# Scaling of the softmax weights moved from VectorE to GpSimd in a two-layer attention kernel

## The chip, the cores and the metric

The kernel runs on one core of a Trainium2 chip. The metric is device time in microseconds, from start to end of one execution; the median of several runs is given. The core has five engines that run at the same time and wait for each other by semaphores: TensorE (PE in the profile; its weight loads are PEld), VectorE (DVE), ScalarE (ACT), GpSimd (POOL) and SyncE (SP), which here issues DMAs.

## What is computed

Two transformer layers on 256 rows of width 1024, in float32. The first layer attends with 16 query heads on 4 key/value heads in three branches (compressed blocks, selected blocks, window), each branch weighted by a gate:

```python
s = jnp.einsum('bqgrd,bgqkd->bgrqk', qc, kg).astype(jnp.float32) * scale
p = masked_softmax(s, msel)
o_sel = jnp.einsum('bgrqk,bgqkd->bqgrd', p.astype(vg.dtype), vg)
...
o = gc[..., 0:1] * o_cmp + gc[..., 1:2] * o_sel + gc[..., 2:3] * o_win
```

With 256 rows the selected branch and the window branch both come down to plain causal attention, with keys and values of their own. The second layer attends with 16 heads, each with its own keys and values, which comes down to causal attention as well. Each attention is followed by an output projection, a residual with layer norm, a gated feed-forward network of width 2816 and a second layer norm.

## The kernel before

All matrix products with weights are done as three products of a high part and a low part of each operand (L1050, `product`). ScalarE rounds each weight unit of 128 x 2048 (L427, through the helper at L420) and VectorE computes what is left of it (`rest_of_unit`, L700, through the helper at L698). Four such units are in flight; the units stream in by SyncE's DMAs. The order of the work on each engine is written out by hand, engine by engine, and the engines meet at counting semaphores.

Each attention runs in jobs: 16 in the first layer (8 pairs of heads, each with the selected and the window branch), 8 in the second (8 pairs of heads). A job handles two heads and both halves of the rows; the first half sees 128 keys, the second 256. So a job's weights are four blocks for each partition, of 128, 128, 256 and 256 columns, 768 in all. `probs` holds two jobs, so does the place of the scores in PSUM. What happens to job i:

- TensorE, `scores` (L1237 and the mask at L1241), after the exponential of job i-2 (`p_ready`)
- VectorE, `row_maxima` (L867): two reductions from PSUM
- ScalarE, `exp` (L561): four exponentials with their sums, after TensorE has turned job i-2 (`pT_done`)
- VectorE, `scale_probs` (L872 to L888): one reciprocal of the sums (L875), a wait for it on VectorE itself (`link`), and four multiplications in place, in the first attention by reciprocal and gate (L883), in the second by the reciprocal (L886)
- TensorE, `turn_probs` (L1252, L1256): six transposes, after `p_scaled`
- ScalarE copies the turned weights from PSUM (L584, shown as L420)
- TensorE, `weigh_values` (L1270, L1273, and in each second job of the first attention a product of the compressed branch, L1267)
- ScalarE and VectorE take the output of a pair of heads from PSUM as high and low part (`outputs_hi`, `outputs_lo`)

In each step i of its loop (L1280) TensorE does the scores of job i+2, then turns job i, then weighs the values of job i-1. In the last two steps there are no scores; twelve products with the output weights stand in their place. VectorE's loop (L902) does the maxima of job i+2, then `scale_probs` of job i+1, then `outputs_lo` of job i-2 where a pair of heads is complete. Ahead of the loop VectorE scales jobs 0 and 1. In the second attention 48 products of the last value projection stand between the scores of job 1 and those of job 2.

GpSimd makes constants at the start, loads the gains of the norms (`load_gain`, L387) and computes the reciprocal root of each variance (`roots`, L391, eight times in all); the rest of the time it waits. Its instructions stand in a fixed order (L401 to L412).

Of the kernel before, what the change touches and what calls it, by code (L numbers as in the profile page):

```python
# [26 lines left out]
HALF = 2  # L27
P = 128
# [26 lines left out]
NSA_JOBS = 16  # L55
MOBA_JOBS = 8
# [3 lines left out]
def build(nc, x_rows, x_cols, stream, w_gates, w1, w2, cpos, positions, norms, out):  # L60
# [4 lines left out]
    ALU = mybir.AluOpType  # L65
# [3 lines left out]
    with ExitStack() as ctx:  # L69
# [3 lines left out]
        def sem(name):  # L73
            return ctx.enter_context(nc.semaphore(name))
# [18 lines left out]
        probs = arena[:, 3072:4608].rearrange("p (b n) -> p b n", b=2)  # L93
# [28 lines left out]
        gates = sb("gates", [P, HALF, NH, 3])  # L122
        neg_max = sb("neg_max", [P, JOBS, HALF, 2])
        sums = sb("sums", [P, JOBS, HALF, 2])
        coef = sb("coef", [P, JOBS, HALF, 2])
# [69 lines left out]
        s_ready = sem("s_ready")  # L195
        max_ready = sem("max_ready")
        p_ready = sem("p_ready")
        p_scaled = sem("p_scaled")
        pT_done = sem("pT_done")
        pT_ready = sem("pT_ready")  # L200
# [141 lines left out]
        @block.gpsimd  # L342
        def _(gp):
            steps = [0]

            def link(ins):

                steps[0] += 1
                ins.then_inc(g_step, 1)
                gp.wait_ge(g_step, steps[0])  # L350

            nc.gpsimd.memset(minus_half[:, :], -0.5).then_inc(warm, 1)
            freqs = np.power(np.float32(THETA), -np.arange(0, ROPE, 2, dtype=np.float32) / np.float32(ROPE))
            for j in range(ROPE // 2):
                nc.gpsimd.memset(inv[:, j:j + 1], float(freqs[j]))
                nc.gpsimd.memset(inv[:, 8 + j:9 + j], float(freqs[j]))
            nc.gpsimd.memset(phase[:, :, 0:8], 0.0)
            nc.gpsimd.memset(phase[:, 0, 8:16], 0.25)
            nc.gpsimd.memset(phase[:, 1, 8:16], math.pi / 2)
            nc.gpsimd.memset(row_ok[:, :], 1.0)  # L360
            nc.gpsimd.memset(own_head[:, :], 1.0)
            nc.gpsimd.memset(causal[:, :, :], 0.0)
            nc.gpsimd.memset(cmp_mask[:, :, :], 0.0)
            nc.gpsimd.memset(hidT[:, :, :, :, :], 0.0)
            nc.gpsimd.memset(kcz[:, :, :, :], 0.0)
            nc.gpsimd.memset(hid_rows[:, :], 0.0)
            nc.gpsimd.memset(ident_b[:, :], 0.0)
            link(nc.gpsimd.memset(ident[:, :], 0.0))
            for m in (ident, ident_b):
                nc.gpsimd.affine_select(out=m[:, :], in_=m[:, :], compare_op=ALU.not_equal, fill=1.0, base=0,  # L370
                                        pattern=[[-1, P]], channel_multiplier=1)

            nc.gpsimd.affine_select(out=causal[:, :, :], in_=causal[:, :, :], compare_op=ALU.is_ge, fill=NEG,
                                    base=0, pattern=[[0, 2], [-1, P]], channel_multiplier=1)

            nc.gpsimd.affine_select(out=cmp_mask[:, :, :], in_=cmp_mask[:, :, :], compare_op=ALU.is_ge, fill=NEG,
                                    base=1 - CB, pattern=[[P, HALF], [-CS, 16]], channel_multiplier=1)

            nc.gpsimd.affine_select(out=row_ok[:, :], in_=row_ok[:, :], compare_op=ALU.is_ge, fill=0.0,
                                    base=1 - CB, pattern=[[P, HALF]], channel_multiplier=1)  # L380

            link(nc.gpsimd.affine_select(out=own_head[:, :], in_=own_head[:, :], compare_op=ALU.is_ge, fill=0.0,
                                         base=0, pattern=[[-16, 8]], channel_multiplier=1))
            nc.gpsimd.affine_select(out=own_head[:, :], in_=own_head[:, :], compare_op=ALU.is_ge, fill=0.0,
                                    base=15, pattern=[[16, 8]], channel_multiplier=-1).then_inc(consts, 1)

            def load_gain(l):  # L387
                gp.dma_start(gain[:, 0, :], norms[l, 0:1, :].to_broadcast([P, D])).then_inc(gain_in, 16)
                gp.dma_start(gain[:, 1, :], norms[l, 1:2, :].to_broadcast([P, D])).then_inc(gain_in, 16)

            def roots(l):  # L391
                for half in range(HALF):
                    gp.wait_ge(var_ready, 2 * l + half + 1)
                    nc.gpsimd.tensor_tensor(rstd[:, l, half:half + 1], var_eps[:, l, half:half + 1],
                                            minus_half[:, :], ALU.pow).then_inc(rstd_ready, 1)

            def rows_done(sets, doubled):
                gp.wait_ge(turned, sets)
                gp.wait_ge(twice_ready, doubled)

            rows_done(Q1 + 1, 2)  # L401
            load_gain(0)
            roots(0)
            gp.wait_ge(x_ready, 4)
            load_gain(1)
            roots(1)
            rows_done(MK1 + 1, 2)
            load_gain(2)
            roots(2)
            gp.wait_ge(x_ready, 12)  # L410
            load_gain(3)
            roots(3)  # L412
# [269 lines left out]
        def _(dve):  # L682
# [3 lines left out]
            def link(ins):  # L686

                steps[0] += 1
                ins.then_inc(v_step, 1)
                dve.wait_ge(v_step, steps[0])  # L690
# [109 lines left out]
            for kv, k in ((0, KC), (1, VC)):  # L800
                dve.wait_ge(turned, k + 1)
                for part in range(2):
                    lo = HD * part
                    src = ps[lo:lo + HD, 4 + 2 * kv:6 + 2 * kv, :].rearrange("p b (g n j) -> p j (b g) n", n=16, j=CS)
                    last = nc.vector.tensor_tensor(
                        blocks[lo:lo + HD, kv, :, :, :], src[:, :, :, part:part + NCMP],
                        cpos_sb[lo:lo + HD, kv, :].unsqueeze(2).unsqueeze(3).to_broadcast([HD, CS, KV, NCMP]), ALU.add)
# [53 lines left out]
            def attend(jobs, job, j0, a0, u):  # L861
                def row_maxima(i):
                    b = i % 2
                    dve.wait_ge(s_ready, j0 + i + 1)
                    for half in range(HALF):
                        keys = P * (half + 1)
                        last = nc.vector.tensor_reduce(  # L867
                            neg_max[:, j0 + i, half, :],
                            ps[:, s_bank(b, 0):s_bank(b, 1) + 1, P * half:P * half + keys], AX.X, ALU.max, negate=True)
                    last.then_inc(max_ready, 1)  # L870

                def scale_probs(i):  # L872

                    dve.wait_ge(p_ready, j0 + i + 1)
                    link(nc.vector.reciprocal(coef[:, j0 + i, :, :], sums[:, j0 + i, :, :]))  # L875
                    for half in range(HALF):
                        keys = P * (half + 1)
                        for h in range(2):
                            at = slice(2 * P * half + h * keys, 2 * P * half + (h + 1) * keys)
                            one_over_sum = coef[:, j0 + i, half, h:h + 1]  # L880
                            if j0 == 0:
                                gate = gates[:, half, i // 2 * 2 + h, 1 + i % 2:2 + i % 2]
                                last = nc.vector.tensor_scalar(probs[:, i % 2, at], probs[:, i % 2, at],  # L883
                                                               one_over_sum, gate, ALU.mult, ALU.mult)
                            else:
                                last = nc.vector.tensor_scalar(probs[:, i % 2, at], probs[:, i % 2, at],  # L886
                                                               one_over_sum, None, ALU.mult)
                    last.then_inc(p_scaled, 1)  # L888

                def outputs_lo(i):  # L890
                    t = job(i)[0]
                    dve.wait_ge(a_hi_ready, a0 + t + 1)
                    minus(a_lo[:, :, t, :], out_ps(t), a_hi[:, :, t, :].bitcast(f32)).then_inc(a_lo_ready, 1)

                row_maxima(0)
                if j0 == 0:
                    rest_to(u + 2)
                row_maxima(1)
                scale_probs(0)
                scale_probs(1)  # L900
                rest_to(u + 2)
                for i in range(jobs):  # L902
                    if i + 2 < jobs:
                        row_maxima(i + 2)
                    if 0 < i and i + 1 < jobs:
                        scale_probs(i + 1)
                    if i >= 2 and job(i - 2)[4]:
                        outputs_lo(i - 2)
                    if i >= jobs - 2:
                        rest_to(u + 3 + i - (jobs - 2))  # L910
                for i in range(jobs - 2, jobs):
                    if job(i)[4]:
                        outputs_lo(i)
# [600 lines left out]
```

## Time and profile before

| | |
|---|---|
| median of 3 runs | 655.66 us (655.51 to 655.67) |
| profiled execution | 655.48 us, of which the span of the trace is 653.7 us |
| TensorE busy | 641.7 us, 98% of the span |
| VectorE busy | 400.3 us, 61% |
| ScalarE busy | 313.3 us, 48% |
| GpSimd busy | 16.3 us, 3% |
| granted clock of TensorE | 0.996 of full speed (2.4 GHz) |
| first attention | from about 79 to 136 us of the span |
| second attention | from about 402 to 440 us |

In the rows below, times are in microseconds from the start of the span unless marked ns. `arena` is the memory that holds `probs` and `probsT`; `ps` is PSUM. "out<-in" gives the tensors that are written and read, with partitions x elements and type; xN is the number of instructions that a row merges. "L883" is line 883 of the kernel. What stands in brackets at the end is the time that the engine was idle before the instruction, and what ended it; "issue" is time in which it waited for nothing that the profile shows. TensorE's products overlap each other, so a duration of one product is longer than its share of the time.

### The profile page before, as it was taken

The page shows a single profiled execution, that of the slowest core. Times are in us where ns is not written, and L with a number is a line of the kernel's source. Part 1 is how long each engine was busy: PE and PEld are TensorE (multiplying, and loading weights), DVE is VectorE, ACT ScalarE, POOL GpSimd, SP SyncE. Part 2 cuts the span into 40 slices and gives each one's busy share as a digit, 9 for nine tenths or more (in the row PEclk, how much of TensorE's full clock was granted, in tenths as well). Part 3 has the DMA queues.
Part 4 walks back from the last instruction along what each step waited for, and adds up shares of the span by engine and source line. Part 5 has one row for each costly group of instructions (what it writes and reads, how often), then busy time and mean ns, then how long its engine had stood idle before and what let it go on. Part 6 is the DMA issues. An engine that isn't in the chain of part 4 may idle for free.

```text
span 653.7 us, 8507 instructions
## 1 busy us (share of the span) xinstructions
PE 641.7 (98%) x3277; PEld 512.8 (78%) x3277; DVE 400.3 (61%) x505; ACT 313.3 (48%) x440; POOL 16.3 (3%) x56
## 2 busy tenths in 40 slices
PE   9999999999999999999999999999999999999995
PEld 6887766687888888888877887778788888888874
DVE  4794688868565445554477755787685445554437
ACT  5663588835443333444443555784263333444420
POOL 2000000001000000000000000000100000000001
PEclk9999999999999999999999999999999999999998
DMA  8993330035574545554533654313566555455301
GB/s 307 394 343 140 128 129 1 3 128 207 207 259 182 189 183 188 192 192 192 189 133 130 257 183 138 129 70 124 195 217 250 185 189 188 192 192 192 128 1 64
DMA packets 18718, 113.03 MB, mean 173 GB/s; under 512 B 2816, under 2 KB 3328, under 8 KB 6016
## 3 DMA queue, kind: packets, MB, share of 16 engines
q1 hardware_dynamic: 16528, 102.65, 42.6%
q10 hardware_dynamic: 1008, 5.77, 2.3%
q0 software_dynamic: 1152, 4.19, 1.9%
q8 instruction: 21, 0.34, 0.2%
q14 instruction: 9, 0.07, 0.0%
HBM read 111.56 MB, written 1.05 MB: 172 GB/s over the span
## 4 chain that ended last, share of the span: by engine, by line
PE 89%; DVE 9%; ACT 2%; issue 0%; DVEq 0%; ACTq 0%
PE ps L1052 25%; PE ps L1054 24%; PE ps L1053 24%; PE ps L1237 3%; DVE w_lo L698 2%; PE ps L1270 2%; PE ps L1252 2%; PE ps L1336 2%; DVE bn L933 1%; DVE x L947 1%; DVE x L928 1%; PE ps L1178 1%; PE ps L1134 1%; PE ps L1241 1%; DVE x L955 1%; PE ps L1119 1%
## 5 line engine op out<-in xcount | busy, mean ns | idle before, releaser
L698 DVE TENSOR_TENSOR w_lo<-raw,w_hi 128x2048 fp32r<-128x2048 f32 (+2 forms) x101 | 220.1, 2185 | 101.7 <-ACT w_hi L420 101.4
L1052 PE MATMUL ps<-w_hi,a_hi 128*128 128x512 f32 x592 | 235.4, 398 | 0.1
L420 ACT ACTIVATE w_hi<-raw 128x2048 fp32r<-128x2048 f32 (+2 forms) x101 | 184.3, 1830 | 97.6 <-PE ps L1054 89.6
L1054 PE MATMUL ps<-w_hi,a_lo 128*128 128x512 f32 x592 | 231.0, 390 | 0.0
L1053 PE MATMUL ps<-w_lo,a_hi 128*128 128x512 f32 x592 | 230.7, 390 | 0.0
L1052 PEld LDWEIGHTS ps<-w_hi,a_hi 128*128 128x128 f32 x592 | 111.3, 188 | 24.1 <-issue 1.5
L1054 PEld LDWEIGHTS ps<-w_hi,a_lo 128*128 128x128 f32 x592 | 111.1, 188 | 23.8
L1053 PEld LDWEIGHTS ps<-w_lo,a_hi 128*128 128x128 f32 x592 | 111.4, 188 | 21.7
L1052 PE MATMUL ps<-w_hi,h_hi 128*128 128x512 f32 x160 | 62.4, 390 | 0.0
L1054 PE MATMUL ps<-w_hi,h_lo 128*128 128x512 f32 x160 | 62.3, 390 | 0.0
L1053 PE MATMUL ps<-w_lo,h_hi 128*128 128x512 f32 x160 | 62.2, 389 | 0.0
L607 ACT ACTIVATE arena<-ps 128x512 f32<-128x512 f32 x18 | 10.8, 599 | 68.3 <-PE ps L1054 68.3
L420 ACT ACTIVATE h_hi<-ps 128x512 fp32r<-128x512 f32 x20 | 12.0, 599 | 60.2 <-PE ps L1336 60.2
L561 ACT ACTIVATE arena<-ps,neg_max 128x128 f32<-128x128 f32 (+1 forms) x96 | 39.5, 448 | 2.3 <-DVE neg_max L867 2.3
L987 DVE TENSOR_TENSOR arena<-arena,ps 128x512 f32<-128x512 f32 x18 | 12.4, 688 | 37.8 <-ACT arena L607 37.8
L1054 PEld LDWEIGHTS ps<-w_hi,h_lo 128*128 128x128 f32 x160 | 30.0, 188 | 6.3
L1052 PEld LDWEIGHTS ps<-w_hi,h_hi 128*128 128x128 f32 x160 | 30.0, 188 | 6.2
L1053 PEld LDWEIGHTS ps<-w_lo,h_hi 128*128 128x128 f32 x160 | 30.0, 188 | 6.2
L420 ACT ACTIVATE arena<-ps 128x768 f32<-128x768 f32 (+2 forms) x28 | 23.6, 847 | 21.4 <-PE ps L1054 12.0
L698 DVE TENSOR_TENSOR h_lo<-ps,h_hi 128x512 fp32r<-128x512 f32 x20 | 13.8, 691 | 28.5 <-ACT h_hi L420 28.5
L867 DVE TENSOR_REDUCE neg_max<-ps 128x2 f32<-128x256 f32 (+1 forms) x48 | 24.4, 553 | 8.0 <-PE ps L1241 7.5
L420 ACT ACTIVATE a_hi<-ps 128x256 fp32r<-128x256 f32 (+1 forms) x28 | 13.8, 501 | 20.0 <-PE ps L1087 17.9
(150 smaller groups left out, 475.5 us busy)
## 6 DMA issues: line engine op xcount, KB each, us to landing
raw<-stream SPq DMA_DIRECT2D x94, 1024.0 KB, 4.8
arena<-w ACTq DMA_DIRECT2D x4, 1024.0 KB, 13.8
rows<-norms POOLq DMA_DIRECT2D x8, 512.0 KB, 4.6
twice<-x_cols SPq DMA_DIRECT2D x4, 256.0 KB, 6.1
raw<-stream SPq DMA_DIRECT2D x2, 512.0 KB, 7.3
x<-x_rows ACTq DMA_DIRECT2D x1, 1024.0 KB, 5.0
out<-x SPq DMA_DIRECT2D x3, 256.0 KB, 2.1
raw<-stream ACTq DMA_DIRECT2D x2, 256.0 KB, 4.3
```

Of the source, the lines that this page charges most:

```text
L420: return nc.scalar.activation(dst, src, ACT.Copy, scale=scale)
L561: last = nc.scalar.activation(probs[:, b, at:at + keys], ps[:, s_bank(b, h), P * half:P * half + keys], ACT.Exp, bias=neg_max[:, j0 + i, h ...
L698: return nc.vector.tensor_tensor(dst, a, b, ALU.subtract)
L867: last = nc.vector.tensor_reduce(neg_max[:, j0 + i, half, :], ps[:, s_bank(b, 0):s_bank(b, 1) + 1, P * half:P * half + keys], AX.X, ALU.ma ...
L987: nc.vector.tensor_tensor(h_rows[:, :, :], silu[:, :, :], ps[:, 0:2, FC:2 * FC], ALU.mult).then_inc(h_ready, 1)
L1052: nc.tensor.matmul(dst, hi, m_hi, start=start, stop=False)
L1053: nc.tensor.matmul(dst, hi, m_lo, start=False, stop=False)
L1054: return nc.tensor.matmul(dst, lo, m_hi, start=False, stop=stop)
L1237: nc.tensor.matmul(ps[:, s_bank(b, h), P * half:P * half + keys], qT[on, q, P * half:P * (half + 1)], kk[on, k, 0:keys], start=half == 0, ...
L1252: nc.tensor.transpose(acc_flat[:, 2048 + P * (2 * h + half):2048 + P * (2 * h + half + 1)], probs[:, b, at:at + P], ident[:, :])
L1270: nc.tensor.matmul(dst[HD * h:HD * (h + 1)], values[:, 0, cols[h]:cols[h] + HD], probsT[:, b, S * h:S * (h + 1)], start=j0 > 0, stop=False)
L1336: last = nc.tensor.transpose(hT_ps[:, half, t, :], h_rows[:, half, P * t:P * (t + 1)], ident[:, :])
```

## The change

A new semaphore `coef_ready` counts reciprocals. VectorE's part of the step becomes `reciprocals`: the same wait for the exponential, the reciprocal, and a signal; the wait of VectorE for its own reciprocal goes. The four multiplications, with the same operands, are now issued by GpSimd in a loop over all jobs of an attention, with one wait for the reciprocal for each job and the signal `p_scaled` at the job's last multiplication. In GpSimd's order they stand after the load of gain 0 and ahead of root 0 in the first attention, and after the load of gain 2 and ahead of root 2 in the second.

```diff
+            def scale_probs(jobs, j0):
+                for i in range(jobs):
+                    gp.wait_ge(coef_ready, j0 + i + 1)
+                    for half in range(HALF):
+                        keys = P * (half + 1)
+                        for h in range(2):
+                            at = slice(2 * P * half + h * keys, 2 * P * half + (h + 1) * keys)
+                            one_over_sum = coef[:, j0 + i, half, h:h + 1]
+                            if j0 == 0:
+                                gate = gates[:, half, i // 2 * 2 + h, 1 + i % 2:2 + i % 2]
+                                last = nc.gpsimd.tensor_scalar(probs[:, i % 2, at], probs[:, i % 2, at],
+                                                               one_over_sum, gate, ALU.mult, ALU.mult)
+                            else:
+                                last = nc.gpsimd.tensor_scalar(probs[:, i % 2, at], probs[:, i % 2, at],
+                                                               one_over_sum, None, ALU.mult)
+                    last.then_inc(p_scaled, 1)
...
             rows_done(Q1 + 1, 2)
             load_gain(0)
+            scale_probs(NSA_JOBS, 0)
             roots(0)
...
             load_gain(2)
+            scale_probs(MOBA_JOBS, NSA_JOBS)
             roots(2)
...
-                def scale_probs(i):
+                def reciprocals(i):
 
                     dve.wait_ge(p_ready, j0 + i + 1)
-                    link(nc.vector.reciprocal(coef[:, j0 + i, :, :], sums[:, j0 + i, :, :]))
...
-                    last.then_inc(p_scaled, 1)
+                    nc.vector.reciprocal(coef[:, j0 + i, :, :], sums[:, j0 + i, :, :]).then_inc(coef_ready, 1)
...
                 row_maxima(1)
-                scale_probs(0)
-                scale_probs(1)
+                reciprocals(0)
+                reciprocals(1)
                 rest_to(u + 2)
                 for i in range(jobs):
                     if i + 2 < jobs:
                         row_maxima(i + 2)
                     if 0 < i and i + 1 < jobs:
-                        scale_probs(i + 1)
+                        reciprocals(i + 1)
```

## Rows read from the trace of the kernel before

**Rows 1.** The page: busy time of each engine, share of the span, instructions.

```profile
PE 641.7 (98%) x3277; PEld 512.8 (78%) x3277; DVE 400.3 (61%) x505; ACT 313.3 (48%) x440; POOL 16.3 (3%) x56
```

**Rows 2.** Busy time by stretch: stretch, its length, each engine, clock, DMA.

```profile
92.34:125.90 33.56, 33.56 (x291) 22.42 (x291) 29.27 (x88) 30.14 (x113) 0.00 (x0) 1.00 0.01 1
419.00:430.70 11.70, 11.70 (x107) 7.75 (x105) 10.52 (x35) 11.70 (x46) 0.00 (x0) 1.00 0.01 4
```

**Rows 3.** Timeline, first attention's middle: start, duration, engine, line, operation.

```profile
102.79 0.93 PE L1237 MATMUL ps<-kk,qT 64*128 64x128 f32 x8
...
103.25 0.42 DVE L698 TENSOR_TENSOR a_lo<-ps,a_hi 128x256 fp32r<-128x256 f32 x1
...
104.08 1.02 DVE L867 TENSOR_REDUCE neg_max<-ps 128x2 f32<-128x256 f32 x2 [0.41 <-PE ps L1241]
...
105.02 0.17 DVE L875 RECIPROCAL coef<-sums 128x4 f32<-128x4 f32 x1
...
105.22 1.25 DVE L883 TENSOR_SCALAR arena<-arena,coef,gates 128x128 f32<-128x128 f32 x4
...
105.42 0.93 PE L1237 MATMUL ps<-kk,qT 64*128 64x128 f32 x8
...
106.52 0.66 PE L1252 MATMUL ps<-ident,arena 128*128 128x128 f32 x4
...
108.56 0.93 PE L1237 MATMUL ps<-kk,qT 64*128 64x128 f32 x8
```

**Rows 4.** Timeline, start of the first attention.

```profile
86.48 1.73 ACT L420 ACTIVATE arena<-ps 128x1024 f32<-128x1024 f32 x2
86.64 0.18 DVE L875 RECIPROCAL coef<-sums 128x4 f32<-128x4 f32 x1 [0.42 <-ACT arena L561]
...
86.85 1.25 DVE L883 TENSOR_SCALAR arena<-arena,coef,gates 128x128 f32<-128x128 f32 x4
...
88.01 1.95 DVE L867 TENSOR_REDUCE neg_max<-ps 128x2 f32<-128x256 f32 x4
...
89.07 0.37 ACT L561 ACTIVATE arena<-ps,neg_max 128x128 f32<-128x128 f32 x1 [0.85 <-DVE neg_max L867]
...
90.82 0.18 DVE L875 RECIPROCAL coef<-sums 128x4 f32<-128x4 f32 x1 [0.86 <-ACT arena L561]
...
92.34 0.66 PE L1252 MATMUL ps<-ident,arena 128*128 128x128 f32 x4 [0.25 <-DVE arena L883]
```

**Rows 5.** Timeline, second attention, jobs 2 to 4.

```profile
419.83 0.18 DVE L875 RECIPROCAL coef<-sums 128x4 f32<-128x4 f32 x1 [0.26 <-ACT arena L561]
...
419.90 0.93 PE L1237 MATMUL ps<-kk,qT 64*128 64x128 f32 x8
...
421.11 0.66 PE L1252 MATMUL ps<-ident,arena 128*128 128x128 f32 x4
```

**Rows 6.** Timeline of GpSimd and the variance before its first root.

```profile
2.27 0.32 POOL L366 MEMSET hid_rows<- 128x256 f32 x1
2.52 0.20 POOL L367 MEMSET ident_b<- 128x128 bf16 x1
2.67 0.20 POOL L368 MEMSET ident<- 128x128 f32 x1
3.11 0.29 POOL L370 TENSOR_SCALAR_AFFINE_SELECT ident<-ident 128x128 f32<-128x128 f32 x1 [0.24 <-POOL ident L368]
3.37 0.29 POOL L370 TENSOR_SCALAR_AFFINE_SELECT ident_b<-ident_b 128x128 bf16<-128x128 bf16 x1
3.62 0.41 POOL L373 TENSOR_SCALAR_AFFINE_SELECT causal<-causal 128x256 bf16<-128x256 bf16 x1
3.98 0.21 POOL L376 TENSOR_SCALAR_AFFINE_SELECT cmp_mask<-cmp_mask 128x32 f32<-128x32 f32 x1
...
143.27 0.15 DVE L940 TENSOR_SCALAR var_eps<-mean_var 128x1 f32<-128x1 f32 x1
...
143.51 1.00 POOL L394 TENSOR_TENSOR rstd<-var_eps,minus_half 128x1 f32<-128x1 f32 x1 [68.08 <-DVE var_eps L940]
```

More of the change, by code:

```diff
@@ L197, in build @@
         p_ready = sem("p_ready")
+        coef_ready = sem("coef_ready")
         p_scaled = sem("p_scaled")
@@ L870, in row_maxima @@
                     last.then_inc(max_ready, 1)
-                def scale_probs(i):
+                def reciprocals(i):
                     dve.wait_ge(p_ready, j0 + i + 1)
-                    link(nc.vector.reciprocal(coef[:, j0 + i, :, :], sums[:, j0 + i, :, :]))
[L876 to L887, printed above, removed]
-                    last.then_inc(p_scaled, 1)
+                    nc.vector.reciprocal(coef[:, j0 + i, :, :], sums[:, j0 + i, :, :]).then_inc(coef_ready, 1)
                 def outputs_lo(i):
```

## The prediction

> **What bounds the kernel now.** I read the busy line of each engine first. TensorE is busy for 641.7 us of the 653.7 us span, 98% [rows 1]. So a change on VectorE or GpSimd pays only where TensorE now waits for it, and costs only where TensorE comes to wait. The change touches the two attention stretches alone. The busy times of stretches say that in the middle of both, TensorE is busy all the time (33.56 of 33.56 us, and 11.70 of 11.70 us), that ScalarE is close to it (30.14, and 11.70), that VectorE has some rest, and that GpSimd does nothing [rows 2]. There is nothing to gain in the middle: the row maxima wait for scores, not the other way round.
>
> The timeline of two jobs in the middle of the first attention shows who waits for whom [rows 3]. Call S(n) the scores of job n, T(n) the turning of its scaled weights, V(n) its weighted values. TensorE runs S(n+1), T(n-1), V(n-2), S(n+2), T(n), in this order. S starts at 102.79, 105.42 and 108.56: periods of 2.63 and 3.14, the longer one with the extra product of the compressed branch in it. T starts 1.10 after its S (105.42 to 106.52), and from T to the next S it is 1.53 (103.89 to 105.42), or 2.04 with the extra product (106.52 to 108.56).
>
> Now the way to T(n) beside TensorE: S(n+1) starts at 102.79, its maxima at 104.08 (1.29 later), the reciprocal of job n at 105.02 to 105.19 (2.40 after S), the four scalings of job n at 105.22 for 1.25, to 106.47. T(n) starts at 106.52, 0.05 later, which is also just when TensorE is done with S(n+2). So every second job of the first attention has a slack of about nothing: this is the place that decides. The other jobs have the 0.5 us that the extra product gives. The reciprocal cannot come sooner, since VectorE puts the maxima of job n+1 ahead of it, and they wait for TensorE.
>
> **The change part by part.** What goes: 96 scalings leave VectorE, 1.25 us a job in the first attention. What comes: a semaphore from VectorE to GpSimd, the same scalings there, and GpSimd's signal to TensorE. The first hop: the variance ends at 143.42 and GpSimd's root starts at 143.51, so 0.09 [rows 6]. For the last hop I take the 0.05 of VectorE. With X for the four scalings of a job on GpSimd, T(n) can start 2.40 + 0.09 + X + 0.05 = 2.54 + X after S(n+1). Now it starts 3.73 after it. So X is covered up to 1.19, call it 1.2 us. Write e = X - 1.2.
>
> In the first attention, when e is above 0, T(n) of an odd job is late. After it come 2.04 to S(n+3), and again 2.54 + X to T(n+2): a pair takes 4.58 + X instead of 5.78, which is e more. The even job between has its slack and rides along. This is one e a pair, not one a job. It holds for T(5), T(7), T(9), T(11) and T(13): 5e. T(3) is set by T(2), below. T(14) and T(15) have twelve matmuls of the output weights ahead of them, and cost nothing.
>
> *Start of the first attention* [rows 4]. Here VectorE is now in the way: scaling job 1 holds it from 86.85 to 88.10, and the maxima of jobs 2 and 3 start only at 88.01. ScalarE's exponential of job 2 starts at 89.07 after 0.85 of waiting; its copies had ended at 86.48 + 1.73 = 88.21. With the scalings gone, the maxima of job 2 can start at 86.82 (after the reciprocal) and end at 87.84, ahead of ScalarE's copies. The exponential then starts at 88.21, 0.86 sooner, and with it the reciprocal of job 2 (90.82 now) and S(4). T(2), now at 92.34, would start at 90.82 - 0.86 + 0.18 + 0.09 + X + 0.05 = 90.28 + X: at X = 1.2 it is 91.48, a gain of 0.86. So the start gives -0.86 + e, once. T(3) then follows T(2) by TensorE's own 2.64. T(0) and T(1) move by up to e as well; S(4) then follows V(0) at about 90.3 + e, and from that side T(2) could start at 91.4 + e, no later than from the other.
>
> *Second attention* [rows 5]. Jobs 0 and 1 are scaled long before T(0), under a block of 48 matmuls. At T(2) VectorE isn't held up by anything: the reciprocal starts at 419.83 because the exponential ended, and the scaling ends just before T(2) at 421.11. Here the hop is pure addition: 419.83 + 0.18 + 0.09 + X + 0.05 = 420.15 + X, at X = 1.2 421.35, a loss of 0.24. T(4) adds another e as above (all periods are short ones here, so T(n) late by e gives T(n+1) its slack back). T(6) and T(7) are covered by matmuls. Together 0.24 + 2e.
>
> *Other queues.* GpSimd's waits stand in order: the gain loads are issued ahead of the scalings as before, its roots come 10 us after the last scaling, so nobody waits for what is queued behind. The 24 new signals from VectorE replace a wait of VectorE on itself. VectorE's output parts come sooner, and TensorE didn't wait for them.
>
> *The price X.* The trace has no tensor_scalar on GpSimd. Its memsets advance by 0.15 us (128 columns) and 0.25 (256), so four such would take 0.15 + 0.15 + 0.25 + 0.32 = 0.87: a floor, since nothing is read. Its selects, which read one tensor and write one, advance by 0.26 and 0.36 and end after 0.41: 0.26 + 0.26 + 0.36 + 0.41 = 1.29 [rows 6]. A select of 128 columns takes 0.29, a memset 0.20: reading one operand adds 0.09. The new scalings read two scalars of each partition from SBUF besides (one in the second attention). My estimate is 0.09 for each: X = 1.29 + 4 x 0.18 = 2.01 in the first attention, 1.29 + 4 x 0.09 = 1.65 in the second. The ceiling is the root: 1.00 for one column, so four of these are 4.0. I stay near the selects, since the ceiling is a power, not a product.
>
> The Trainium skill (GPSIMD Engine Reference, § Performance pitfalls for Q7 kernels) puts about 102 cycles on each read command, which at its 1.2 GHz is 0.085 us; the trace's 0.09 between select and memset agrees. Its opening speaks against the change as a whole: for elementwise arithmetic VectorE is roughly twice as fast. By that, X would be 2 x 1.25 = 2.5; no row here shows it, and the sum would be that of rival (b) at its near edge.
>
> **The sum.** First attention: e = 0.81, -0.86 + 0.81 + 5 x 0.81 = +4.0. Second: e = 0.45, 0.24 + 0.9 = +1.1. Together +5.1 us. The profiled execution took 655.48 us with 1.8 around its span; the median of the runs shown is 655.66, 0.18 above. On the median: 660.8 us.
>
> With one X for both, the change is -0.62 + 8e. Ends: X = 0.87 gives e = -0.33. Then the middle is TensorE's own, and so is the start from T(1) on, at 88.10 by T(0) after S(2): T(2) comes at 91.3, a gain of 1.0. The second attention gains 0.1 (S(4) is the limit): -1.1 in all, 654.5. X = 4.0 gives 8 x 2.8 - 0.6 = +21.8; GpSimd's own queue, 4.1 a job, is not yet worse than that.
>
> **The rivals.** (a) GpSimd is as quick as its selects or quicker, the two scalars cost nothing: X from 0.87 to 1.44. At 1.29 the sum is +0.1, 655.8 us; at 1.2 it is 655.0. The start's gain then pays for the second attention's hop. This is the case on the other side: its place is T(2) of the first attention, its price 0.86, and it decides as long as e stays under 0.08. For it: both select rows, and a single pass over one tensor. Against it: the fixed 0.09 for an operand.
>
> (b) Arithmetic on GpSimd costs twice VectorE's 1.25 or more: X from 2.5 to 4.0. At X = 2.5 the sum is -0.6 + 10.4 = +9.8, 665.4 us; at 4.0 it is 677.5. For it: the root at 1.00 us for one column, a large fixed price. Against it: that is a power, and the selects are not dear.
>
> (c) The two engines exclude each other at SBUF. The output part of VectorE (0.42 us at 103.25 [rows 3]) follows right behind each second reciprocal, so exactly beside a scaling. In the first attention it falls on the even jobs, whose 0.5 covers it only if X is small; at my X it would move them by up to 0.42 + 0.81 - 0.50 = 0.73, which the next odd job then has as slack. In the second it comes with jobs 3 and later and adds about 0.4. Some 1 us in all, to 661.8: inside my range. The Trainium skill (SBUF — State Buffer, § Who interferes with whom) holds only VectorE instructions with two SBUF inputs or in a 2-port mode to block GpSimd; the output part has one input from PSUM. By that rule (c) costs nothing, and only the rests of whole weight units (two SBUF inputs) count, which fall where matmuls cover them.
>
> (d) The diff does what it says: no wait of VectorE for the scaled weights remains, so I give no chance to a change without effect.
>
> **How the numbers follow.** My case (X from 1.44 to 2.5, with or without (c)): 0.55. Rival (a): 0.28. Rival (b): 0.17. What a measurement of this kernel can tell from no change is about 0.2%, 1.3 us; it is crossed at e = 0.24, X = 1.44, upwards. Downwards no X reaches it: 0.03, taken out of (a), stands for a use of VectorE's free time that I don't see. So faster 0.03, within 0.25, slower 0.72. The range starts at 655.0, the X at which the cover just holds, which leaves out the lower part of (a), and goes to 668.0, X = 2.8, which takes in the near half of (b).
>
> **What would show it.** GpSimd rows of 128 and 256 columns near 0.45 and 0.57 us (no stretch where they are 0.3 and 0.4). TensorE's L1252 released by GpSimd in every second job, S to S twice summing to 4.6 + X rather than 5.78. The maxima of job 2 at about 86.8, T(2) at 90.3 + X. VectorE idle most of each job. I am wrong if L1252 never waits (X below 1.2), if it waits in every job by the whole of e, or if the pair of periods grows while X is below 1.2, which would mean a longer hop.

## The result, and the profile after

The changed kernel takes 664.07 us (median of 4 runs, 663.78 to 665.49) against 655.65 us for the kernel before: a ratio of 1.0133, with a 95% interval of 1.0121 to 1.0146. It is 8.4 us slower. One of the four runs, at 665.49, had a mean granted clock of 0.994, the other three 0.997. The forecast was 660.8 us with a range of 655.0 to 668.0: the sign and the range hold; 5.1 us were forecast and 8.4 measured.

The page of the kernel after: busy time, and the chain that ended last by engine. GpSimd, which was busy for 16.3 us [rows 1] and in neither attention, now has 76.7 us and 3% of the chain.

```profile
PE 643.4 (97%) x3277; PEld 512.6 (77%) x3277; DVE 372.9 (56%) x409; ACT 313.6 (47%) x440; POOL 76.7 (12%) x152
...
PE 84%; DVE 9%; POOL 3%; ACT 2%; issue 1%; DMA 1%; DVEq 0%; ACTq 0%
```

Busy time by stretch: T(2) to T(13) of the first attention, and the second attention from 420 to 436 us. TensorE, busy all the time before [rows 2], is busy for 32.66 of 35.49 us and for 12.61 of 16.00 us. VectorE, relieved, only became idle.

```profile
92.84:128.33 35.49, 32.66 (x274) 20.91 (x274) 13.91 (x40) 28.09 (x106) 21.39 (x44) 1.00 0.00 1
...
420.00:436.00 16.00, 12.61 (x110) 8.10 (x112) 6.60 (x17) 11.78 (x41) 11.30 (x17) 1.00 0.21 89
```

GpSimd's scalings by line and shape (line, engine, operation, count, busy us, mean ns): first the first attention's form (L408, reciprocal and gate) over the whole span, then the second's (L411, reciprocal alone) from 424 to 438 us, where nothing disturbs them.

```profile
L408 POOL TENSOR_SCALAR arena<-arena,coef,gates 128x256 f32<-128x256 f32 x32 | 17.4, 553 | 0.0
...
L408 POOL TENSOR_SCALAR arena<-arena,coef,gates 128x128 f32<-128x128 f32 x32 | 14.0, 446 | 27.2 <-DVE coef L895 27.2
```

```profile
L411 POOL TENSOR_SCALAR arena<-arena,coef 128x256 f32<-128x256 f32 x8 | 7.3, 922 | 0.0
L411 POOL TENSOR_SCALAR arena<-arena,coef 128x128 f32<-128x128 f32 x8 | 4.7, 602 | 4.7 <-DVE coef L895 4.7
```

The form with *less* arithmetic takes longer. The four scalings of a job take 1.95 us in the first attention and 2.97 in the second (5.94 for two jobs back to back). Over the whole span the mean of the second's short ones is 0.85 and that of the long ones 1.02, the numbers that the expectations below go by: a few instructions that VectorE blocked are in those means (see the last section).

Where the 8.4 us lie is read from GpSimd's first root of each norm. It starts at 148.00 instead of 143.51 after the first attention; the profiled execution was already 0.16 later before the first scaling (the maxima of job 0 at 80.79 instead of 80.63), so the first attention costs 4.33 us. Between the fourth root and the fifth it is 104.96 us (351.96 to 456.92) instead of 100.78 (347.50 to 448.28): the second costs 4.18. Together that is 8.51.

Some 0.35 us come back in a place that the change does not touch. Behind the sixth root (463.12 before, 471.76 after), VectorE's next step of the norm starts 1.70 us after the root in the kernel before and 1.36 after it in the changed one. At the other seven roots it is 1.34 or 1.35 in both.

```profile
464.82 1.42 DVE L955 SCALAR_TENSOR_TENSOR x<-x,rstd,rows 128x512 f32<-128x512 f32 x2 [0.46 <-DVE x L947]
```

```profile
473.12 1.41 DVE L962 SCALAR_TENSOR_TENSOR x<-x,rstd,rows 128x512 f32<-128x512 f32 x2
```

From the sixth root to the seventh it takes 179.25 us before and 178.91 after. All ten kernels of this document that scale the first attention on GpSimd, wholly or in part, take 178.9; the one other experiment on the kernel before ("early half alone", below) takes 179.27. The cause was not found. So 0.35 us are in the total time of each of the ten when it is compared with the kernel before.

### The profile page after: what moved, and what is told of

Same layout as the page of the kernel before. It is cut to its first block, busy times and chain, and to the rows that moved or that the text cites. A ratio compares the mean times of both kernels' runs of the same rounds, so it can differ in the third digit from the quotient of the medians.

```text
span 662.1 us, 8507 instructions
## 1 busy us (share of the span) xinstructions
PE 643.4 (97%) x3277; PEld 512.6 (77%) x3277; DVE 372.9 (56%) x409; ACT 313.6 (47%) x440; POOL 76.7 (12%) x152
## 4 chain that ended last, share of the span: by engine, by line
PE 84%; DVE 9%; POOL 3%; ACT 2%; issue 1%; DMA 1%; DVEq 0%; ACTq 0%
PE ps L1059 24%; PE ps L1061 24%; PE ps L1060 24%; DVE w_lo L718 2%; POOL arena L408 2%; PE ps L1343 2%; PE ps L1244 1%; POOL arena L411 1%; PE ps L1259 1%; DVE bn L940 1%; DVE neg_max L887 1%; PE ps L1277 1%; DVE x L954 1%; DVE x L935 1%; PE ps L1185 1%; DVE x L962 1%
## 5 line engine op out<-in xcount | busy, mean ns | idle before, releaser
L395 POOL TENSOR_TENSOR rstd<-var_eps,minus_half 128x1 f32<-128x1 f32 x8 | 8.0, 995 | 415.9 <-DVE var_eps L947 415.9
L408 POOL TENSOR_SCALAR arena<-arena,coef,gates 128x128 f32<-128x128 f32 (+1 forms) x64 | 31.1, 499 | 27.2 <-DVE coef L895 27.2
```

Source lines behind the costliest of these rows:

```text
L408: last = nc.gpsimd.tensor_scalar(probs[:, i % 2, at], probs[:, i % 2, at], one_over_sum, gate, ALU.mult, ALU.mult)
```

## The experiments

Each kernel was timed beside the kernel before, which took 655.57 to 655.64 us. "Changed kernel" means the one above, and every diff is against it unless it says otherwise.

### Each attention by itself

In the first run, the second attention's scalings go back to VectorE; the first attention stays on GpSimd.

```diff
-            scale_probs(MOBA_JOBS, NSA_JOBS)
...
+                    if j0 == 0:
+                        nc.vector.reciprocal(coef[:, j0 + i, :, :], sums[:, j0 + i, :, :]).then_inc(coef_ready, 1)
+                        return
+                    link(nc.vector.reciprocal(coef[:, j0 + i, :, :], sums[:, j0 + i, :, :]))
...
```

> The scalings of the first attention on GpSimd, those of the second back on VectorE. My theory: the two attentions cost separately, 4.3 us in the first (variance of the first norm 4.49 us later, less 0.16 of an offset at the start) and 4.2 in the second. So 655.65 + 4.3 = 660.0 us. Rival: part of the cost lies outside them, in a later stage that the shift disturbs; then the sum would not split so, and this kernel would be off 660.0 by over 0.5 us.

Measured: 659.54 us (659.43 to 659.61), 3.9 above the kernel before, ratio 1.0059 (1.0043 to 1.0076). The root stands at 147.91 in its profile, 4.40 later than before, and the second attention is back at 100.73 us between its roots (351.85 to 452.58). So the costs of the two attentions are separate. The time is 0.46 us below the 660.0 that were expected, just inside the 0.5 allowed, and the 0.35 gained behind the sixth root is most of that: a small part of the difference does lie outside the attentions, as a gain.

### Why the second attention's scalings are slow

Three kernels change nothing but the form of the instruction. The first two give the second attention a second multiplication, by a column of ones read from SBUF or by a constant in the instruction.

```diff
-                                                               one_over_sum, None, ALU.mult)
+                                                               one_over_sum, ones[:, 0:1], ALU.mult, ALU.mult)
...
-                                                               one_over_sum, None, ALU.mult)
+                                                               one_over_sum, 1.0, ALU.mult, ALU.mult)
```

> As the changed kernel, but in the second attention each scaling has a second multiplication, by a column of ones read as a scalar of each partition. Theory 'form': GpSimd runs the form with one operation slower (0.85 and 1.02 us) than the form with two (0.45 and 0.55); the added operation makes it faster, X falls from 2.97 to 1.95, and the second attention costs 0.24 + 2 x 0.75 = 1.7 instead of 4.2 us: 661.6 us. Rival 'stage': something of the second attention slows GpSimd; then its rows stay at 0.85 and 1.02 or rise, and the time is 664.1 or more.

> As the run with the column of ones, but the second factor is the constant 1.0 in the instruction. Theory 'two operations are the quick form': rows at 0.45 and 0.55 or 0.09 less each, since one scalar fewer is read; 661.0 to 661.6 us. Rival 'both factors have to be pointers to be quick': rows at 0.85 and 1.02, 664.1 us.

The third takes the gate out of the first attention.

```diff
-                                                               one_over_sum, gate, ALU.mult, ALU.mult)
+                                                               one_over_sum, None, ALU.mult)
```

> As the changed kernel, but the first attention leaves the gate out, so its scalings have one operation as in the second (the branches are then not weighted by their gates). Theory 'form': rows of 0.85 and 1.02 in the first attention too, X = 2.97; a pair of jobs takes 4.58 + 2.97 = 7.55 instead of 6.53, five pairs 5.1 more, the start about 1.5 more, the two longer turns of GpSimd's own queue some more: 671 us. Rival 'stage': rows stay at 0.45 and 0.55 or fall by 0.09 for the scalar that isn't read; 664.1 down to 662.

Measured: 661.36 us (661.24 to 661.55) with the column, 660.73 (660.65 to 660.82) with the constant, 672.79 (671.84 to 673.73) without the gate. The first is inside what was expected, the second 0.3 us below it. The groups by line and shape, first of the kernel with the constant 1.0 (second attention):

```profile
L411 POOL TENSOR_SCALAR arena<-arena,coef 128x256 f32<-128x256 f32 x16 | 7.4, 477 | 0.0
L411 POOL TENSOR_SCALAR arena<-arena,coef 128x128 f32<-128x128 f32 x16 | 5.7, 370 | 18.8 <-DVE coef L895 18.8
```

and then of the kernel without the gate (first attention):

```profile
L407 POOL TENSOR_SCALAR arena<-arena,coef 128x256 f32<-128x256 f32 x32 | 30.9, 979 | 0.0
L407 POOL TENSOR_SCALAR arena<-arena,coef 128x128 f32<-128x128 f32 x32 | 19.0, 606 | 21.6 <-DVE coef L894 21.6
```

The added multiplication makes the instruction 1.6 times (0.602 to 0.370) and 1.9 times (0.922 to 0.477) faster, and taking one out makes the first attention's as slow as the second's had been; four advance by 2.99 us there. So the form decides, not the stage. From 128 to 256 columns the two-operation form grows by 0.107 us, 0.84 ns a column, and the one-operation form by 0.32 us, 2.5 ns a column; extended to no column, an estimate, 0.26 and 0.28 are left. It is the price of a column that differs. With the constant, four scalings take 1.62 us; with the column of ones 1.96, the same as with the gates. The difference, 0.34 for four instructions, is the price of reading one more scalar of each partition: 0.085 each, where the prediction took 0.09 [rows 6]. Why GpSimd is slower at one operation than at two was not found; no run here looks inside it.

The run without the gate is 1.8 us above what was expected of it. Its four times fall in two groups: 671.84 and 671.96 us at a mean granted clock of 0.998, 673.61 and 673.73 at 0.995. The profile is of the 673.61. Busy time of stretches of it, three pairs of jobs and a part of the middle one; the last column but two is the granted clock.

```profile
110.87:118.44 7.57, 5.93 (x54) 3.83 (x50) 2.52 (x7) 5.12 (x20) 5.95 (x9) 1.00 0.00 0
118.44:127.58 9.14, 7.49 (x54) 4.70 (x50) 2.52 (x7) 5.11 (x20) 5.94 (x8) 0.81 0.01 3
122.00:125.00 3.00, 3.00 (x16) 1.64 (x14) 0.00 (x0) 2.30 (x9) 2.38 (x4) 0.50 0.03 8
127.58:135.15 7.57, 5.92 (x55) 3.84 (x50) 2.52 (x7) 5.12 (x20) 5.95 (x8) 1.00 0.00 0
```

The granted clock is 0.50 of full speed, 1.2 GHz, for about 3.4 us from 121.9. TensorE had waited for GpSimd for 1.65 us until 121.48. The pairs around it have waits of the same length (5.93 and 5.92 us busy of 7.57) at full clock, so a wait of this size does not always bring the fall. GpSimd's scalings, 7.57 us apart from pair to pair, are 9.14 apart there: 1.6 us, once. No other trace of this document has such a fall inside an attention. In the two executions at 0.998 it is presumably missing; they lie 0.9 us above what was expected, and that part is not explained.

### The order on VectorE

The kernel with the constant, and VectorE's loop takes the reciprocal first.

```diff
+                    if 0 < i and i + 1 < jobs:
+                        reciprocals(i + 1)
                     if i + 2 < jobs:
                         row_maxima(i + 2)
-                    if 0 < i and i + 1 < jobs:
-                        reciprocals(i + 1)
```

> The kernel with the constant 1.0 (660.7 us), and VectorE's loop takes the reciprocal of job i+1 ahead of the maxima of job i+2 instead of behind them; nothing is added or left out. My theory of the place that decides: T(n) is late because the reciprocal waits behind the maxima of the next job, which wait for TensorE. With the reciprocal first, T(n) can start 0.04 + 0.17 + 0.09 + X + 0.05 after the exponential of job n, about 2.3 at X = 1.95, and the pair of jobs in the first attention falls from 6.53 to between 5.85 and 6.06 us; the maxima come later, which costs the second attention up to 0.4 a job. 658.2 to 659.2 us. Rival: the length of the scalings on GpSimd alone sets the pair, whatever the order on VectorE; then the pair stays at 6.53 and the time at 660.7 or above it.

Measured: 657.19 us (657.09 to 657.88), 3.5 us below the same kernel with the old order, and 1.0 below the lower end of what was expected. Timeline of this kernel in the middle of the first attention:

```profile
104.52 0.60 PE L1259 MATMUL ps<-ident,arena 128*128 128x128 f32 x4
...
104.96 0.18 DVE L895 RECIPROCAL coef<-sums 128x4 f32<-128x4 f32 x1 [1.46 <-ACT arena L581]
105.05 0.99 DVE L887 TENSOR_REDUCE neg_max<-ps 128x2 f32<-128x256 f32 x2
105.23 1.96 POOL L408 TENSOR_SCALAR arena<-arena,coef,gates 128x128 f32<-128x128 f32 x4 [0.91 <-DVE coef L895]
...
107.25 0.66 PE L1259 MATMUL ps<-ident,arena 128*128 128x128 f32 x4
```

The reciprocal is released by ScalarE's exponential, not by the maxima, and 1.96 us on GpSimd end at 107.19, before T. T comes at 101.41, 107.25, 113.02 and 118.85: 5.81 a pair on average, where it was 6.53 in the changed kernel. The first attention then costs 0.67 us (root at 144.25, less 0.07 of offset) instead of 4.35. So most of the cost of the first attention can be had back with GpSimd as slow as it is. It hung on where GpSimd's work began: behind a reduction that waits for TensorE. The expected price in the second attention, 0.4 a job, was too high: it costs 1.30 between its roots (348.21 to 450.29), with the old order 1.10.

### Both engines at once

Each job's scalings are divided: those of 128 columns on GpSimd (in the second attention with the column of ones as second factor), those of 256 on VectorE; TensorE waits for both.

```diff
-                    for half in range(HALF):
+                    for half in range(1):
                         keys = P * (half + 1)
                         for h in range(2):
...
+                    dve.wait_ge(coef_ready, j0 + i + 1)
+                    for h in range(2):
+                        at = slice(2 * P + h * 2 * P, 2 * P + (h + 1) * 2 * P)
...
+                    last.then_inc(p_scaled_v, 1)
```

> Each job's four scalings are split: the two of 128 columns on GpSimd (two operations each, 0.45 us), the two of 256 columns on VectorE (0.41 us each), both at the same time. Theory 'they run beside each other': T(n) can start 2.40 + 0.09 + 0.87 + 0.05 = 3.41 after S(n+1), earlier than now with all on VectorE (3.73), so nothing is late and the start of the first attention gains some 0.3 us: 655.2 us. Rival 'they exclude each other at SBUF' (rival c of the prediction): rows of one of them stretch to the sum, 0.87 + 0.82, T(n) comes 0.5 late once a pair, 655.6 + 3 to 4 = 659 us.

Measured: 654.52 us (654.26 to 655.14), ratio 0.9982 (0.9973 to 0.9992): 1.1 us faster than the kernel before, and 0.7 faster than expected. By the roots it gains 0.94 us in the first attention, where 0.3 was expected, and loses 0.19 in the second (100.97 between its roots); the 0.35 behind the sixth root makes up the rest. Timeline of one job of this kernel:

```profile
104.44 0.17 DVE L898 RECIPROCAL coef<-sums 128x4 f32<-128x4 f32 x1
...
104.64 0.79 DVE L905 TENSOR_SCALAR arena<-arena,coef,gates 128x256 f32<-128x256 f32 x2
104.70 1.04 POOL L411 TENSOR_SCALAR arena<-arena,coef,gates 128x128 f32<-128x128 f32 x2 [2.02 <-DVE coef L898]
...
105.93 0.60 PE L1275 MATMUL ps<-ident,arena 128*128 128x128 f32 x4
```

They do run beside each other, but not freely: two scalings of 128 columns take 1.04 on GpSimd here, where two of the changed kernel would take 0.89, while VectorE's two take 0.79 as ever. GpSimd lost 0.15 of 0.79 us, not all of it, and both end before T. T follows its S by 1.09 (104.84 to 105.93), TensorE's own time.

Two more kernels keep the division in the first attention only, the second of them with an early half of the maxima of job 2; a third divides both attentions, with the constant in the second; a fourth is the kernel before with the early half alone.

```diff
                 reciprocals(0)
+                if j0 == 0:
+                    row_maxima(2, (0,))
                 reciprocals(1)
...
-                        row_maxima(i + 2)
+                        row_maxima(i + 2, (1,) if j0 + i == 0 else (0, 1))
```

> The split of the run before (128 columns on GpSimd, 256 on VectorE) in the first attention only; the second has all scalings on VectorE as in the kernel before the change. The split gained 0.9 us in the first attention and lost 0.2 in the second by the places of the roots, so 655.6 - 1.1 = 654.5 or a little less. Rival: the gain of 1.1 came from somewhere else in the kernel (the second attention, code positions); then this is back above 655.

> As the split in the first attention only, and in its start VectorE takes the first half of the maxima of job 2 (128 keys, 0.36 us) ahead of the reciprocal of job 1, where it is idle for 0.87 us. The exponential of job 2 then starts 0.3 us sooner (the copies on ScalarE end 0.4 us before it starts now): 0.3 us less than the run without it, about 654.2. Rival: the products on TensorE after T(1) take over as the limit, and nothing changes.

> The split in both attentions, with the early half of the maxima, and in the second attention the constant 1.0 as the second factor (0.37 us an instruction of 128 columns instead of 0.45). T(2) of the second attention can come at most 0.1 us sooner than in the kernel before. Expected within 0.2 us of the split in the first attention only with the early half: 654.1 to 654.4.

> The kernel before the change, all scalings on VectorE, with the early half of the maxima of job 2 as the only edit. VectorE is idle 0.42 us before the reciprocal of job 1 and takes the half there; the maxima of job 2 end some 0.25 us sooner, so 655.4. If it gave the whole gain, GpSimd's part in the split would be worth nothing; theory says 655.4, well above 654.2.

| kernel | median, us | ratio to before (95%) | first attention, us |
|---|---|---|---|
| divided, first attention | 654.24 | 0.9982 (0.9973 to 0.9991) | -0.94 |
| the same, early half | 654.04 | 0.9977 (0.9968 to 0.9986) | -1.20 |
| divided in both, early half | 654.00 | 0.9976 (0.9967 to 0.9985) | -1.21 |
| early half alone | 655.35 | 0.9996 (0.9987 to 1.0005) | -0.25 |

The last column is the start of the first root less 143.51 and less the offset at the maxima of job 0, of one profile each. All four are within 0.3 us of what was expected. The three divided kernels are 1.3 to 1.6 us below the kernel before; 0.9 to 1.2 of that lie in the first attention, where the early half alone gives 0.25, so this part needs both engines. Another 0.35 is the shorter step behind the sixth root, which the kernel with the early half alone does not have, so its time by itself would make the part of the division look larger than it is. The intervals of the first three overlap: their order is not established by the times. The profile of the second shows the mechanism at the start: the exponential of job 2 follows ScalarE's copies without a wait, where it waited 0.85 before [rows 4].

```profile
86.44 0.42 DVE L889 TENSOR_REDUCE neg_max<-ps 128x2 f32<-128x256 f32 x1 [0.61 <-PE ps L1267]
...
87.71 1.61 DVE L889 TENSOR_REDUCE neg_max<-ps 128x2 f32<-128x512 f32 x3
88.41 0.37 ACT L583 ACTIVATE arena<-ps,neg_max 128x128 f32<-128x128 f32 x1
```

The best versions are about 1.6 us, 0.24%, below the kernel before, 1.2 of it by what was changed in the first attention.

## Why the prediction was right, and where its size was off

**The place that decides: right.** Timeline of the changed kernel, answering [rows 3]:

```profile
104.24 0.93 PE L1244 MATMUL ps<-kk,qT 64*128 64x128 f32 x8
...
105.53 1.02 DVE L887 TENSOR_REDUCE neg_max<-ps 128x2 f32<-128x256 f32 x2 [2.27 <-PE ps L1248]
...
106.46 0.17 DVE L895 RECIPROCAL coef<-sums 128x4 f32<-128x4 f32 x1
...
106.73 1.94 POOL L408 TENSOR_SCALAR arena<-arena,coef,gates 128x128 f32<-128x128 f32 x4 [1.74 <-DVE coef L895]
106.87 0.93 PE L1244 MATMUL ps<-kk,qT 64*128 64x128 f32 x8
...
108.73 0.66 PE L1259 MATMUL ps<-ident,arena 128*128 128x128 f32 x4 [0.61 <-POOL arena L408]
```

S(n+1) at 104.24, T(n) at 108.73: 4.49 = 2.54 + 1.95, to the hundredth the sum of the prediction, both hops included. The next S of its kind comes at 110.77, so the pair takes 6.53 = 4.58 + 1.95. TensorE waits for GpSimd in every second job and the other rides along. T(3) to T(13) took 28.80 us before (95.04 to 123.84) and take 32.67 (95.66 to 128.33): 3.87 for the five, where the forecast had 4.05. The run with the reciprocal first shows it from the other side.

**The price X of the first attention: right.** 1.95 instead of 2.01, by one operand's 0.09 read off the selects and memsets [rows 6]. The Trainium skill's price of a read command (GPSIMD Engine Reference, § Performance pitfalls for Q7 kernels), about 102 cycles, an estimate of 0.085 us at its 1.2 GHz, agrees with the 0.085 between the runs with the column and the constant. The factor of roughly two that the same page gives VectorE for elementwise arithmetic (its opening) would have given 2.5; measured is 1.95 against VectorE's 1.25, so 1.6 times.

**The price X of the second attention: the term that failed.** I priced the instruction by what it has to read and do, so the one with one scalar and one multiplication had to be cheaper: 1.65. It is 2.97, where VectorE took 1.01. With the second operation added, the same place takes 1.62, close to the forecast, and the whole kernel 660.73 us, 3.3 below the changed kernel. So the excess over the forecast is this term. That 660.73 is 5.1 above the kernel before, just the forecast's sum, is in part luck: by the roots the first attention costs 4.35 instead of 4.0 and the second 1.10, and 0.35 comes back behind the sixth root. Timeline of the second attention in the changed kernel, answering [rows 5]:

```profile
424.28 0.18 DVE L895 RECIPROCAL coef<-sums 128x4 f32<-128x4 f32 x1 [0.25 <-ACT arena L581]
...
424.55 5.93 POOL L411 TENSOR_SCALAR arena<-arena,coef 128x128 f32<-128x128 f32 x8 [3.51 <-DVE coef L895]
...
426.86 0.42 DVE L718 TENSOR_TENSOR a_lo<-ps,a_hi 128x256 fp32r<-128x256 f32 x1
...
427.58 0.66 PE L1259 MATMUL ps<-ident,arena 128*128 128x128 f32 x4 [1.98 <-POOL arena L411]
...
429.18 0.93 PE L1244 MATMUL ps<-kk,qT 64*128 64x128 f32 x8
...
430.54 0.66 PE L1259 MATMUL ps<-ident,arena 128*128 128x128 f32 x4
...
434.70 0.66 PE L1259 MATMUL ps<-ident,arena 128*128 128x128 f32 x4 [1.31 <-POOL arena L411]
...
437.66 0.66 PE L1259 MATMUL ps<-ident,arena 128*128 128x128 f32 x4
```

These are T(2), T(3), T(4) and T(5), with S(5) at 429.18. T(4) and T(5) in the kernel before:

```profile
426.43 0.60 PE L1252 MATMUL ps<-ident,arena 128*128 128x128 f32 x4
...
429.07 0.60 PE L1252 MATMUL ps<-ident,arena 128*128 128x128 f32 x4
```

The mechanism with the measured price: 0.24 + 2 x 1.77 = 3.8, measured 4.18. The reciprocal of job 2 starts 4.45 later than before (424.28, 419.83). With that taken off, T(2) is late by 2.02, which is 0.24 + 1.77, and T(4) by 3.82, another 1.80. Most of the remaining 0.4 is a wait the prediction dismissed: GpSimd's own queue. Two jobs come back to back (5.93), 2.97 each against the 2.64 that TensorE took from T(4) to T(5). T(3) is late by 0.27 more for that, but T(4) hangs on T(2) through S(5) and does not feel it. T(5) is late by 0.32 more, and that stays: 4.14.

**The start of the first attention: half right.** The maxima of job 2 come at 86.88, as forecast, but bring only half of the gain:

```profile
88.11 0.81 ACT L440 ACTIVATE arena<-ps 128x768 f32<-128x768 f32 x1 [0.45 <-PE ps L1263]
88.82 0.36 ACT L581 ACTIVATE arena<-ps,neg_max 128x128 f32<-128x128 f32 x1
...
92.84 0.66 PE L1259 MATMUL ps<-ident,arena 128*128 128x128 f32 x4 [0.43 <-POOL arena L408]
```

ScalarE's copy of job 0 stands ahead of the exponential of job 2 and waits for T(0), which GpSimd made late by 0.8. I had written that T(0) and T(1) move by up to e, and had followed that along TensorE but not along ScalarE. With 0.16 of offset taken off, the exponential starts at 88.66, which is 0.41 sooner than before (89.07 [rows 4]) but not the 0.86 sooner of the forecast (88.21). T(2) starts at 92.68 instead of the 92.23 that follows for X = 1.95. So 0.45 of the gain of 0.86 was given back: T(2) is 0.34 later than before, forecast was about 0.05 earlier.

**The cases.** It fell in my case for the first attention and, by its X of 2.97, in rival (b) for the second: one change, two prices. What (b) gave as its reason, a large fixed price, did not show: by the estimate above 0.28 us an instruction is fixed, and the column is dear. Rival (a) was wrong, since the two scalars do cost. Rival (c) in the form given there is refuted: the output part of VectorE (0.40 us, at 109.18) and the scalings at 109.37 overlap for 0.21 us, and these take 1.95 as all others; in the second attention the output part at 426.86 lies wholly inside eight scalings that take 5.93, twice 2.97. What the rule of the Trainium skill (SBUF — State Buffer, § Who interferes with whom) does name showed up, below.

## What to carry to other kernels

A step that moves to an idle engine is paid on the path from its release to its consumer, plus a hop, and not by the engine's share of time; look first at what releases it, since here an order change on VectorE gave back most of what a slower engine had cost in the first attention. Price each form of an instruction on the engine by itself, and take no form for cheaper because it does less. Dividing a short step between two engines is worth trying where moving it isn't. Before a gain of a few tenths of a microsecond is put down to a change, look whether a stage that the change does not touch has moved as well.

## What the runs showed of the hardware

- On GpSimd, a multiplication by one scalar with no second operation takes 0.60 us for 128 columns and 0.92 for 256. With a second operation by a constant it takes 0.37 and 0.48, by a second scalar from SBUF 0.45 and 0.55. I had not expected less work to cost more.
- GpSimd and VectorE block each other where VectorE reads two operands from SBUF for long. In the kernel with the column of ones, the second attention's first two jobs lie beside VectorE's rests of two weight units:

```profile
411.04 8.06 POOL L413 TENSOR_SCALAR arena<-arena,coef,ones 128x128 f32<-128x128 f32 x8 [3.10 <-DVE coef L897]
```

```profile
414.17 4.58 DVE L720 TENSOR_TENSOR w_lo<-raw,w_hi 128x2048 fp32r<-128x2048 f32 x2 [1.63 <-ACT w_hi L442]
```

  Eight scalings take 8.06 us instead of 3.92: an instruction of GpSimd ended only after both rests (at 419.10 and 418.75). With the constant, the eight are done in 3.22 us before the rests begin. In the changed kernel it went the other way round as well: one rest, at 133.50, took 2.56 us instead of 2.29 beside a scaling already under way. The Trainium skill's rule (SBUF — State Buffer, § Who interferes with whom) fits these: VectorE reads two inputs from SBUF there. By the same section one side also blocks the other for the whole instruction where VectorE is in a 2-port mode. The division of jobs shows a loss of 0.15 us beside 0.79, and whether VectorE was in such a mode is not shown by any run here. All of it was covered by TensorE's work, though at T(7) of the second attention by little: GpSimd ended at 446.33, T(7) started at 446.57.
- TensorE's granted clock fell to 0.50 for about 3.4 us in one execution of the kernel without the gate, behind a wait of 1.65 us, and cost 1.6 us there. The same waits a pair of jobs earlier and later had full clock.
